# Two new orders in a decoder layer: the first products of both feed-forward networks, and the preparation of heads in latent attention

## The reference, cut to what matters

```python
def rms_norm(x, gain):
    y = xf * lax.rsqrt(jnp.mean(xf * xf, axis=-1, keepdims=True) + EPS)
    return (y * gain)
def swiglu_ffn(u, w_gu, w_down):
    g, up = jnp.split(u @ w_gu, 2, axis=-1)
    return (jax.nn.silu(g) * up) @ w_down
...
    q = split_heads(rms_norm(c_q, mla_cq_norm) @ mla_w_uq, MLA_HEADS)
    kv = split_heads(rms_norm(c_kv, mla_ckv_norm) @ mla_w_ukv, MLA_HEADS)
    ...
    q = rms_norm(q, mla_q_norm)
    k = rms_norm(k, mla_k_norm)
    q = jnp.concatenate([q[..., :64], rope(q[..., 64:], cos, sin)], axis=-1)
    ...
    o_mla = merge_heads(block_causal_attention(q, k, v)) @ w_branch_mla
    g_fox, g_mla = jnp.split(jax.nn.sigmoid(gate_logit + b_gate), 2, axis=-1)
    return (g_fox * o_fox + g_mla * o_mla) @ w_out
...
h = h + 0.5 * swiglu_ffn(rms_norm(h, ffn1_norm), ffn1_w_gu, ffn1_w_down)
h = h + token_mixing(rms_norm(h, mix_norm), ...)
h = h + 0.5 * swiglu_ffn(rms_norm(h, ffn2_norm), ffn2_w_gu, ffn2_w_down)
```

## Time and profile before

| | us |
|---|---|
| median of 3 runs (2532.12 to 2543.33) | 2540.17 |
| the profiled execution | 2539.42 |
| its span | 2537.6 |
| TensorE busy in the span | 2395.9 (94%) |
| VectorE | 1423.5 (56%) |
| ScalarE | 958.0 (38%) |
| GpSimd | 508.5 (20%) |

### The profile page before, as it was taken

One profiled execution on the slowest core, in us unless ns is written; L12 is line 12 of the kernel. 1 busy time (PEld: TensorE's weight loads), 2 busy tenths in 40 slices (PEclk: granted clock), 3 DMA queues, 4 the chain that ended last, 5 costly groups with the idle time before them and its releaser, 6 DMA issues. The chain is left out here.

```text
span 2537.6 us, 36864 instructions
## 1 busy us (share of the span) xinstructions
PE 2395.9 (94%) x14060; PEld 2124.4 (84%) x14060; DVE 1423.5 (56%) x2057; ACT 958.0 (38%) x1621; POOL 508.5 (20%) x632
## 2 busy tenths in 40 slices
PE   6899999999978999989899999989989999999999
PEld 6899999999968888878677777778877888887887
DVE  7655655655554574572455555544276666556553
ACT  5333333333334454442343333353343333334332
POOL 0032300000022442440233333332410332000000
PEclk8999999999988899989999999989999999999999
DMA  5356633375421000001111111023613656427553
GB/s 187 119 190 216 208 127 105 145 273 184 144 83 52 26 1 25 26 1 36 37 50 37 37 40 36 26 96 132 237 54 132 226 192 213 139 69 276 207 200 109
DMA packets 132698, 297.99 MB, mean 117 GB/s; under 512 B 10096, under 2 KB 57072, under 8 KB 129216
## 3 DMA queue, kind: packets, MB, share of 16 engines
q1 hardware_dynamic: 132544, 295.88, 33.6%
HBM read 206.99 MB, written 88.72 MB: 117 GB/s over the span
## 5 line engine op out<-in xcount | busy, mean ns | idle before, releaser
L1070 DVE TENSOR_TENSOR f_w_lo<-f_rw,f_w_hi 128x1024 fp32r<-128x1024 f32 x154 | 195.2, 1267 | 222.2 <-ACT f_w_hi L590 222.2
L833 PE MATMUL f_ps<-u_hi,f_w_hi 128*128 128x260 f32 (+1 forms) x1056 | 283.7, 323 | 25.9 <-DVE f_w_lo L1070 13.1
L833 PE MATMUL f_ps<-u_lo,f_w_hi 128*128 128x260 f32 (+1 forms) x1056 | 283.0, 323 | 0.0
L833 PE MATMUL f_ps<-u_hi,f_w_lo 128*128 128x260 f32 (+1 forms) x1056 | 282.7, 322 | 0.0
L590 ACT CAST f_w_hi<-f_rw 128x1024 fp32r<-128x1024 f32 x154 | 161.2, 1047 | 164.4 <-PE f_ps L833 157.2
L833 PE MATMUL f_ps<-f_far_hi,f_w_hi 128*128 128x260 f32 (+1 forms) x792 | 211.9, 322 | 8.7 <-DVE f_ev L1086 8.7
L833 PEld LDWEIGHTS f_ps<-u_hi,f_w_hi 128*128 128x128 f32 x1056 | 178.3, 192 | 42.2 <-DVE f_w_lo L1070 14.6
L833 PE MATMUL f_ps<-f_far_lo,f_w_hi 128*128 128x260 f32 (+1 forms) x792 | 210.9, 321 | 0.0
L833 PE MATMUL f_ps<-f_far_hi,f_w_lo 128*128 128x260 f32 (+1 forms) x792 | 210.7, 321 | 0.0
L833 PEld LDWEIGHTS f_ps<-u_lo,f_w_hi 128*128 128x128 f32 x1056 | 177.8, 192 | 14.3
L833 PEld LDWEIGHTS f_ps<-u_hi,f_w_lo 128*128 128x128 f32 x1056 | 177.7, 192 | 14.1
(11 more groups left out here) (392 smaller groups left out, 5954.0 us busy)
## 6 DMA issues: line engine op xcount, KB each, us to landing
f_rw<-in_gu SPq DMA_DIRECT2D x88, 512.0 KB, 4.4
f_rw<-kept_dsum SPq DMA_DIRECT2D x32, 704.0 KB, 4.7
f_rw<-kept_hid SPq DMA_DIRECT2D x33, 520.0 KB, 5.6
f_rw<-in_down SPq DMA_DIRECT2D x24, 704.0 KB, 4.3
f_rw<-kept_hid SPq DMA_DIRECT2D x33, 512.0 KB, 5.4
h_in<-in_wd SPq DMA_DIRECT2D x11, 1024.0 KB, 6.7
kept_dsum<-h_in SPq DMA_DIRECT2D x44, 256.0 KB, 3.0
h_out<-in_wd SPq DMA_DIRECT2D x11, 1024.0 KB, 7.2
```

Of the source, the lines that this page charges most:

```text
L833: last = nc.tensor.matmul(out[:, b, 0:N], w[:, c], u[:, b * N:(b + 1) * N], start=(j < 3 and k == 0 and i == 0), stop=(k == 3 and i == 2), ...
L1070: nc.vector.tensor_tensor(slot(w_lo, st), src, slot(w_hi, st).bitcast(F32), ALU.subtract).then_inc(wlo_done, 1)
```

## The change

No operation is added, removed or changed in size; some are split into two functions and called at other places.

**Networks.** In the first network the gains are loaded behind the first tile of x rather than the fourth, and VectorE waits for them after its row copies. TensorE spreads the first roots before the transposes of tiles 4 and 5, and puts the first half of product 0 before the transposes of tile 7. ScalarE's row copies, casts and squares are in another order. In both networks the rest of pass 0 is written out on ScalarE and VectorE to step 4, and the loop starts at step 5: both halves of product 2 are snapped together, `weight_hi` and `weight_lo` of steps 5 and 6 come before the casts of product 6.

**Latent attention.** In the loop TensorE does `broadcast(w - 1)` before `weigh` and `sums(w)` after it. On ScalarE the copy to `rs` comes before the roots. On VectorE `mean_squares(w)` goes from before the hi part of the weights to behind it, `split_lo` and `scale`; the turning of the query (`turn`) is a step of its own behind `mean_squares`. In head 0 each unit goes through in one step: projection, gate groups, sums, gate groups, broadcast, then scaling and turning, and its split one step later instead of three. `FIRST` and `COPY_FIRST` are new.

```diff
             def start_from_rows():
...
-                for t in range(4):
+                load_rows(0)
+                sp.dma_start(g.gains[:, :], g.dram["gains"]).then_inc(start.gains_in, 16)
+                for t in range(1, 4):
                     load_rows(t)
-                sp.dma_start(g.gains[:, :], g.dram["gains"]).then_inc(start.gains_in, 16)
@@ ScalarE, first network, behind spread_copy(0)
+                rows_kept(10)
+                rows_kept(11)
+                both(0)
                 rows_squared(4)
                 rows_squared(5)
-                both(0)
-                rows_kept(10)
-                rows_kept(11)
+                rows_kept(12)
+                rows_kept(13)
                 rows_squared(6)
-                rows_kept(12)
+                both(1)
                 rows_squared(7)
-                rows_kept(13)
                 roots(1)
-                both(1)
                 weight_hi(1)
             else:
...
                 square_of(2 * KD - 1)
+                weight_hi(2)
                 roots(1)
             spread_copy(1)
+            if first:
+                weight_hi(2)
             snap(0, 0)
-            weight_hi(2)
             snap(0, 1)
             both(2)
             weight_hi(3)
             both(3)
             silu(1, 0)
+            both(4)
             silu(1, 1)
-            both(4)
             weight_hi(4)
             snap(2, 0)
+            snap(2, 1)
+            snap(3, 0)
             both(5)
+            weight_hi(5)
+            snap(3, 1)
+            weight_hi(6)
             both(6)
-            for st in range(3, STEPS):
+            silu(4, 0)
+            for st in range(5, STEPS):
@@ TensorE, first network
+                spread_roots(0)
                 rows_turned(4)
                 rows_turned(5)
-                spread_roots(0)
                 rows_turned(6)
+                product(0, 0)
                 rows_turned(7)
-                product(0, 0)
                 product(0, 1)
@@ VectorE, both networks
             if first:
-                dve.wait_ge(start.gains_in, 16)
...
                 weight_lo(0)
+                dve.wait_ge(start.gains_in, 16)
...
             if first:
                 weight_mix(2)
+            else:
+                weight_lo(2)
+                weight_mix(3)
             scaled(0, 1)
             mix_first()
+            if first:
+                weight_lo(2)
             both_lo(2)
-            weight_lo(2)
-            weight_mix(3)
+            if first:
+                weight_mix(3)
             scaled(1, 1)
+            weight_lo(3)
             mix_second()
             evacuate(1, 0)
             both_lo(3)
-            weight_lo(3)
+            evacuate(1, 1)
             weight_mix(4)
-            evacuate(1, 1)
             both_lo(4)
             weight_lo(4)
             mix_third()
             weight_mix(5)
             both_lo(5)
+            weight_lo(5)
             mix_fourth()
             both_lo(6)
-            for st in range(3, STEPS):
+            weight_lo(6)
+            evacuate(4, 0)
+            for st in range(5, STEPS):
@@ latent attention
-        FIRST = {(w, x): 2 if 2 <= w < 6 else 1 - x if w >= 6 else 0 for w in range(14) for x in range(2)}
-        FIRST.update({(0, 0): 1, (0, 1): 5, (1, 0): 2})
+        FIRST = {(w, x): 0 for w in range(-1, 14) for x in range(2)}
+        FIRST.update({(-1, 0): 1, (-1, 1): 4, (0, 0): 1, (0, 1): 2, (5, 0): 1, (5, 1): 1})
+        FIRST.update({(w, x): 1 + 2 * x for w in range(1, 5) for x in range(2)})
+        FIRST.update({(w, 0): 1 for w in range(8, 14)})
-        COPY_FIRST = (2, 4, 6, 13)
+        COPY_FIRST = (0, 2, 4, 13)
@@ ScalarE, loop (early is split_hi(w - 3); late was root, then spread(w - 1), then values_hi)
                     exponential(p, h, w)
                     if more:
                         square(p, h + 1, w)
-                        late(p, h + 1, w)
+                        spread(p, h + 1, w - 1)
+                        root(p, h + 1, w)
+                        values_hi(p, h + 1, w)
@@ ScalarE, head 0
             for w in range(NW):
-                early(0, 0, w)
+                split_hi(0, 0, w - 1)
+                square(0, 0, w)
+                root(0, 0, w)
                 copy_logits(0, 0, w, COPY_FIRST)
-                square(0, 0, w)
-                late(0, 0, w)
+                spread(0, 0, w)
+                values_hi(0, 0, w)
@@ TensorE, loop (sums(w) and broadcast(w - 1) go out of prepare)
+                    if more and 1 <= w <= NU:
+                        broadcast(p, h + 1, w - 1)
                     if shifted(p, h, w):
                         weigh(p, *shifted(p, h, w))
+                    if more and w < NU:
+                        sums(p, h + 1, w)
                     if more:
                         prepare(p, h + 1, w)
@@ TensorE, head 0
-            gates(0, 0, 0, 0, FIRST)
+            gates(0, 0, -1, 0, FIRST)
             latent_sum(pe, 8)
-            gates(0, 0, 0, 1, FIRST)
-            products(0, 0, 0)
-            prepare(0, 0, 0)
-            for w in range(1, NW):
+            gates(0, 0, -1, 1, FIRST)
+            for w in range(NU):
+                products(0, 0, w)
+                gates(0, 0, w, 0, FIRST)
+                sums(0, 0, w)
+                gates(0, 0, w, 1, FIRST)
+                broadcast(0, 0, w)
+            for w in range(NU, NW):
                 maxima(0, 0, w, 0)
-                if w < NU:
-                    products(0, 0, w)
                 gates(0, 0, w, 0, FIRST)
                 maxima(0, 0, w, 1)
-                gates(0, 0, w, 1, FIRST)
                 prepare(0, 0, w)
@@ VectorE (mean_squares goes out of early; scale loses the three turning operations to turn)
+            def roots(p, h, w):
+                if 0 <= w - 3 < NU:
+                    split_lo(p, h, w - 3)
+                if 1 <= w <= NU:
+                    scale(p, h, w - 1)
+                if w < NU:
+                    mean_squares(p, h, w)
+                if 1 <= w <= NU:
+                    turn(p, h, w - 1)
+
+            def first_roots(w):
+                if w < NU:
+                    mean_squares(0, 0, w)
+                if 1 <= w <= NU:
+                    split_lo(0, 0, w - 1)
+                if w < NU:
+                    scale(0, 0, w)
+                    turn(0, 0, w)
...
                     nc.vector.tensor_copy(p_hi[:, w % 2, 0:n], p32[:, w % 2, 0:n]).then_inc(phi_done, 1)
                     if more:
+                        roots(p, h + 1, w)
                         prepare(p, h + 1, w)
...
             for w in range(NW):
                 early(0, 0, w)
+                first_roots(w)
                 prepare(0, 0, w)
```

More of the change, by code:

```diff
@@ L2327, in _, with split_hi @@
         def _(act):
-            def early(p, h, w):
-                u = w - 3
+            def split_hi(p, h, u):
                 if 0 <= u < NU:
@@ L2351, in square, with root @@
                                              ACT.Square).then_inc(squared, 1)
-            def late(p, h, w):
+            def root(p, h, w):
                 if w < NU:
@@ L2359, in late, with spread @@
                     nc.scalar.activation(r0[:, w % 2, :], r0[:, w % 2, :], ACT.Exp, scale=-0.5).then_inc(rooted, 1)
-                if 1 <= w <= NU:
-                    u = w - 1
+            def spread(p, h, u):
+                if 0 <= u < NU:
                     n = QK_TOKENS[units[u][1]][1]
@@ L2365, in late, with values_hi @@
                     nc.scalar.copy(rs[:, 0:n], BC[:, 0:n]).then_inc(rs_done, 1)
+            def values_hi(p, h, w):
                 if w == V_STEP:
@@ L2405, in head @@
                     if more:
-                        early(p, h + 1, w)
+                        split_hi(p, h + 1, w - 3)
                         copy_logits(p, h + 1, w)
@@ L2565, in prepare @@
             def prepare(p, h, w):
-                if w < NU:
-                    sums(p, h, w)
-                if 1 <= w <= NU:
-                    broadcast(p, h, w - 1)
                 maxima(p, h, w, 2)
@@ L2637, in scale, with turn @@
                                                    rs[:, 0:n], ALU.mult, ALU.mult).then_inc(x_done, 1)
+                else:
+                    nc.vector.tensor_tensor(x[ROPE_ROWS], g.turn[0:ROPE, t0:t0 + n], rs[0:ROPE, 0:n], ALU.mult)
+                    nc.vector.scalar_tensor_tensor(x[0:NOPE], src[0:NOPE, 0:n], g.gains[0:NOPE, g.MK_COL:g.MK_COL + 1],
+                                                   rs[0:NOPE, 0:n], ALU.mult, ALU.mult).then_inc(x_done, 1)
+            def turn(p, h, u):
+                is_q, c = units[u]
+                t0, n = QK_TOKENS[c]
+                x = x32[:, u % 2, 0:n]
+                if is_q:
                     upto(dve, x_done, NU, p, h, u + 1)
@@ L2646, in scale @@
                                             ALU.add).then_inc(rope_steps, 1)
-                else:
```

(10 more changed lines are left out.)

## The result

| | us |
|---|---|
| changed kernel, median of 20 runs (2537.23 to 2557.41) | 2548.39 |
| kernel before, median of 20 runs (2530.90 to 2544.12) | 2539.32 |
| ratio, 95% interval | 1.0042, 1.0029 to 1.0055 |
| profiled execution of the changed kernel, its span | 2543.42, 2541.6 |

The changed kernel is about 10 us slower: 9.1 by the two medians, 10.7 by the ratio. Both networks did what I forecast, rather more; the latent attention lost four times what I had given it.

What follows compares the result with a forecast made beforehand. Only stretches where TensorE stands still were taken to pay. Gains of 5.6 and 3.9 us in the networks less 2.4 and 2.5 in the latent attention gave 4.6 us, a median of 2535.5; range 2518 to 2548.

Steps and rivals of the forecast that it cites:

- The networks: Both feed-forward networks: seventh product starts earlier; net 5.6 us gained in the first, 3.9 in the second.
- the restart at half rate: TensorE behind its new wait before the seventh product: half clock rate costs some 2.3 us, 2.4 in the second network.
- The third rival: Networks give half: the addition before the seventh product or silu's table load is later; 5 of 9.5 us gone, 2540.5; chance 0.08.
- The first head: First latent head's preparation: net 2.4 us lost, bounds 7.5 gained to 5 lost with the clock down twice.
- The cast behind the turning: First head: ScalarE's cast waits for VectorE's turning before the next square; 4.6 us from broadcast to sums behind a query unit.
- For the clock [...] I add 1: First head: new pauses of nearly 3 us may lower TensorE's clock once, priced at 1 us.
- What follows is bound by the maxima on VectorE and keeps its length within 0.2: First head, behind the sixth broadcast: the stretch keeps its length within 0.2 us.
- The loop: Loop over the other seven heads: 15.0 us of scaling waits go, new ones come; net 2.5 us lost, bounds 15.0 gained to 9 lost.
- step 3 opens 0.35 later: Loop, each head: late mean square delays roots, head end, cast and logits copy, so step 3 opens 0.35 us later.
- Step 6: Loop, each head: a copy of logits behind step 5's roots costs 0.9 us less the broadcast already moved (0.28).
- The rival that waits go and none take their place: Latent attention: waits vanish without replacement; whole it gives 32 us, 2508, half of the latent part 2520; chance 0.2.
- The rival of GpSimd held by VectorE: Latent attention: VectorE's turning stretches GpSimd's Newton steps, delaying the broadcast; 9 us slower, 2544.5; chance 0.2.

Runs made afterwards that it cites:

- Run 5: The changed kernel with ScalarE's copy of the logits for loop steps 3 and 6 moved ahead of the roots, behind the preceding rs copy: 2522.25 us, ratio 0.9939.
- best_turn: Run 5 with the first head in its old order, plus the turning of the fifth unit moved one step later: 2530.74 us, ratio 0.9973.
- best_ms5: Run 5, first head in old order; at step 5 alone mean square ahead of the hi part, roots ahead of the early copy: 2510.22 us, ratio 0.9891.
- run 7: The changed kernel, but in the first latent head ScalarE squares unit w before it casts unit w-1: 2537.97 us, ratio 1.0003.

## Why the prediction was wrong

- **The networks: right.** 9.5 us forecast, 10.7 by the stretches, 11 to 14 by the medians. The chain over VectorE came out 1 us early at its start and 1 more on its way; the restart at half rate was there, at a granted clock of 0.50. The third rival, half the gain, is out.
- **The first head: right in mechanism, too small in size.** The cast behind the turning and the places of the pauses were as described. The steps that failed are two: "For the clock [...] I add 1", and "What follows is bound by the maxima on VectorE and keeps its length within 0.2". Counted from the start of the phase, the sixth broadcast came 3.6 us later than in the kernel before, where my sum without the clock has 1.2; the 2.4 between are the two steps at 0.76 and 0.77. The stretch behind it to the next head's first sums took 19.8 us instead of 16.9, at a clock of 0.79 instead of 1.00. So 6.5 us by the profile where I had 2.4, with 5 as the bound.
- **The loop: the sentence that failed** is "step 3 opens 0.35 later". The gate group opened 0.55 later behind the sums, and the whole step grew by 0.8 to 0.9 us at full clock (7.04 against 6.16 to 6.25). What I did not draw is the other side: with the 0.8 us wait for the scaling gone, TensorE arrives earlier too, and the two short pauses of 0.82 and 0.22 us become one of 1.93. And the term that I put at nothing is the clock. Five of six later heads ran slow behind that pause, and took 8.2 to 8.7 us from the third to the fourth sums; one had the same pause of 1.93 and no fall, and took the 7.04. So the clock is worth 1.2 to 1.7 us a head there, more than the rest of the step's loss. Step 6 (a wait of 1.0 us for the copy) was forecast at its size, but behind it too the clock was lower in two heads, 1.3 us each. Together that is some 9.5 us of this profile, an estimate from these differences. Forecast 2.5 lost (the terms that I wrote out add up to 0.38 a head, not 0.4 to 0.5, which changes little), 9 as the bound; 13 to 16 measured.
- **The rival that waits go and none take their place** had 0.2. Run 5 shows that much of it was one copy on ScalarE away: with it moved the loop gains 1.5 of the 2.1 us a head, and the time is 2522, where this rival had 2508 whole and 2520 for half of the latent part.
- **The rival of GpSimd held by VectorE** gave a time on the right side by a cause that wasn't it. Newton steps of 0.4 to 0.6 us stand in the changed kernel (49 of 168 were over 0.3 us, against 36 before), yet TensorE waited 0.2 us for their result in the whole loop: they were hidden behind the copy. Run 5 uncovers a wait of 1.1 us a head for their result. Without the stretching it was 0.48 (`best_turn`); with the mean square earlier it was all but gone (`best_ms5`, 0.2 us in the whole loop), though two of the four steps still took 0.3 to 0.45. So stretching and lateness both have a part in it. By the Trainium skill ("SBUF — State Buffer", shared port pair) this exclusion is to be expected, and the stretched rows of both engines agree with it; it decided nothing here.
- **The size of it all**: the measured 0.4% lies within the 0.5% that I gave 0.76, but on the other side of the kernel before, and as a time it is just outside the range of 2518 to 2548. Of the 20 us that the latent part lost, against 4.9 forecast, the clock behind the pauses is the greater part by an estimate from these stretches: 5.3 in the first head (2.4 and 2.9) and some 9.5 in the loop.

## What to carry to other kernels

When a change takes a wait away, work out when the engine now arrives at the next one, not only when that one opens: two short waits can merge into a long one, and here TensorE's clock was lower behind the long one in five of six heads, which cost more than the wait had grown. An in-order engine that serves two chains (here ScalarE: the roots, and the copy that frees the logits' bank) wants each piece placed by who waits for it; the same copy moved ahead of the roots gained 26 us where the rs copy stood before it and lost 27, in the old order, where it stood behind. A fix for a named wait is proved only by the stretch behind it: `best_turn` more than halved its wait and made the kernel 17 us slower.

## What the runs showed of the hardware

The pause of 1.93 us was followed by a lower clock in most heads, the seven of 1.0 to 1.1 us in run 5 by none: the mean granted clock of its loop is 1.00. But the length of the pause alone doesn't decide. In the changed kernel pauses of 1.04 and 1.03 us, in two heads at step 6, were followed by 3.5 us at 0.54 and 0.53, and in the first head of the kernel before a pause of 1.92 us by 7.0 us at 1.00:

```profile
1510.65:1514.15 3.50, 3.50 (x12) 2.88 (x13) 1.51 (x3) 1.07 (x3) 2.43 (x4) 0.54 0.65 219
1572.14:1575.64 3.50, 3.50 (x12) 2.86 (x13) 1.48 (x3) 1.06 (x3) 2.40 (x4) 0.53 0.70 220
```

```profile
1217.68:1224.68 7.00, 5.49 (x27) 4.14 (x28) 2.32 (x6) 1.97 (x6) 1.02 (x4) 1.00 0.01 5
```

What else decides isn't shown here, so a forecast needs the fall as a chance with a price, not as a yes or no. In run 7 a pause of 1.59 us was followed by 13 us at 0.50 to 0.51, with TensorE counted busy for 12 of them; one of 1.52 us earlier in the same run was followed by 3.5 us at 1.00. And the exclusion works both ways: a VectorE product of two tensors that takes 0.43 us elsewhere took 1.35 beside a GpSimd subtraction of 1.54 us. VectorE and GpSimd in `best_turn`:

```profile
1322.38 1.35 DVE L2671 TENSOR_TENSOR mla_x<-turn,mla_rs 32x272 f32<-32x272 f32 x1
```

```profile
1321.89 1.54 POOL L2327 TENSOR_TENSOR mla_p_lo<-mla_p,mla_p_hi 128x512 fp32r<-128x512 f32 x1 [0.36 <-DVE mla_p_hi L2777]
```
